# A kernel of 31 stages: one gathering of the five engines between two stages instead of two

## What is computed

```python
for l in range(2):
    h = rmsnorm(y, norm_mix_pre[l])
    m = mixer_ab(h) if l == 0 else mixer_cd(h)        # SSD heads + sparse attention / gated DeltaNet + dilated attention
    y = y + rmsnorm(m, norm_mix_post[l])
    y = y + rmsnorm(sq_relu_mlp(rmsnorm(y, norm_mlp_pre[l]), mlp_w1[l], mlp_w2[l]), norm_mlp_post[l])
```

## Time and profile before

| What | us |
|---|---|
| Median of three runs | 3000.59 |
| Lowest and highest of them | 2994.78, 3001.04 |
| Span of the profiled execution (first to last instruction) | 2999.4 |
| PE busy | 2651.9 (88%) |
| DVE, ACT, POOL busy | 1246.4, 951.2, 903.1 |
| Mean granted share of the TensorE clock | 0.927 |

### The profile page before, as it was taken

One profiled execution on the slowest core, in us unless ns is written; L12 is line 12 of the kernel. 1 busy time (PEld: TensorE's weight loads), 2 busy tenths in 40 slices (PEclk: granted clock), 3 DMA queues, 4 the chain that ended last, 5 costly groups with the idle time before them and its releaser, 6 DMA issues. The chain is left out here.

```text
span 2999.4 us, 47285 instructions
## 1 busy us (share of the span) xinstructions
PE 2651.9 (88%) x19663; PEld 2400.3 (80%) x19663; DVE 1246.4 (42%) x2527; ACT 951.2 (32%) x1755; POOL 903.1 (30%) x453
## 2 busy tenths in 40 slices
PE   5877889888889999978978897889998889899998
PEld 5745888555889999977967696779996569899997
DVE  5655411576343222252654365551105453522224
ACT  4242221364343212152432243222214543412122
POOL 2241221132254333352333133323330003533331
PEclk9978989898999999988988898889999889899998
DMA  4202255451122222222211020112322262122221
GB/s 147 74 15 77 82 93 129 141 214 58 43 71 71 85 85 85 85 74 62 71 31 30 17 76 26 31 30 73 104 73 73 60 185 89 60 85 77 79 84 60
DMA packets 217570, 232.93 MB, mean 78 GB/s; under 512 B 40780, under 2 KB 186668, under 8 KB 216750
## 3 DMA queue, kind: packets, MB, share of 16 engines
q1 hardware_dynamic: 215278, 229.66, 25.1%
q10 hardware_dynamic: 2080, 0.25, 0.1%
HBM read 207.93 MB, written 48.35 MB: 85 GB/s over the span
## 5 line engine op out<-in xcount | busy, mean ns | idle before, releaser
L271 POOL TENSOR_TENSOR WRr<-WR,WH 128x2048 fp32r<-128x2048 f32 (+3 forms) x98 | 438.3, 4472 | 855.0 <-ACT WH L259 855.0
L2231 PE MATMUL PS<-HHr,WRr 128*128 128x288 f32 x1104 | 327.7, 297 | 0.0
L411 PE MATMUL PS<-HHr,WH 128*128 128x288 f32 (+1 forms) x928 | 280.2, 302 | 41.9 <-PEq L97 41.9
L411 PE MATMUL PS<-YTr,WRr 128*128 128x288 f32 x1024 | 304.1, 297 | 0.0
L259 ACT CAST WH<-WR 128x2048 fp32r<-128x2048 f32 (+3 forms) x98 | 180.3, 1840 | 339.1 <-DMA WR<-in_mlp_w 187.6
L411 PE MATMUL PS<-YTr,lt_WX 128*128 128x288 f32 x1408 | 281.8, 295 | 0.0
L411 PE MATMUL PS<-HTr,WH 128*128 128x288 f32 (+1 forms) x928 | 278.1, 300 | 0.0
L411 PE MATMUL PS<-HHr,WRr 128*128 128x288 f32 (+1 forms) x928 | 278.0, 300 | 0.0
L271 POOL TENSOR_TENSOR WRr<-WR,lt_WX 128x2048 fp32r<-128x2048 f32 x35 | 162.1, 4630 | 234.0 <-ACT lt_WX L259 234.0
L411 PE MATMUL PS<-WH,HHr 128*128 128x256 f32 (+3 forms) x760 | 220.1, 290 | 13.0 <-PEq L97 13.0
L411 PEld LDWEIGHTS PS<-YTr,lt_WX 128*128 128x128 f32 x1408 | 227.1, 188 | 0.1
(11 more groups left out here) (672 smaller groups left out, 6145.6 us busy)
## 6 DMA issues: line engine op xcount, KB each, us to landing
WR<-in_mlp_w SPq DMA_DIRECT2D x64, 1024.0 KB, 5.3
WR<-in_cd_w_in SPq DMA_DIRECT2D x34, 1024.0 KB, 5.4
out_dil_s<-in_cache_dil_kv SPq DMA_DIRECT2D x2, 7936.0 KB
WR<-in_ab_w_in SPq DMA_DIRECT2D x10, 1024.0 KB, 5.4
past_rows<-in_cache_nsa_kv SPq DMA_DIRECT2D x16, 256.0 KB, 3.4
WR<-in_ab_w_in SPq DMA_DIRECT2D x16, 256.0 KB, 4.3
WR<-in_nsa_ck_w SPq DMA_DIRECT2D x4, 1024.0 KB, 5.6
WR<-in_nsa_cv_w SPq DMA_DIRECT2D x4, 1024.0 KB, 5.4
```

The costliest lines, as they stand in the source:

```text
L271: pool.tensor_tensor(K.WRr[:, n % RING, 0:used], K.WR[:, n % RING, 0:used], high_slot(K, i, used).bitcast(F32), ALU.subtract).then_inc(K.l ...
L411: last = pe.matmul(out, a, b, start=(n == 0), stop=(n == 3 * len(terms) - 1))
L2231: last = pe.matmul(out, a[:, k, c], h[:, k, x], start=(n == 0), stop=(n == 3 * KT - 1))
```

## The change

The clearing of a stage's semaphores moves from its end to the beginning of the next stage, after that stage has allocated its own, so the two sets never share one. The barrier behind the clearing goes. The block is opened without the option `no_gpsimd_drain`, so POOL drains too when the engines gather at its end. Behind the last stage the last set is cleared and one more barrier stands there, as before.

```diff
+SPENT = []
+
+
+def clear_spent(nc):
+    if SPENT:
+        nc.clear_and_free_semaphores(list(SPENT))
+        SPENT.clear()
+
+
 @contextmanager
 def stage(nc, *names):
     at = nc.next_id()
     sems = [nc.alloc_semaphore(f"{name}_{at}") for name in names]
-    with nc.Block(no_gpsimd_drain=True) as block:
+    clear_spent(nc)
+    with nc.Block() as block:
         yield (block, *sems)
-    nc.clear_and_free_semaphores(sems)
-    nc.all_engine_barrier()
+    SPENT.extend(sems)
...
 def build(nc, K, upto=99):
+    SPENT.clear()
     with ExitStack() as ctx:
...
         with stage(nc, "y_done") as (block, y_done):
...
                 for n in range(K.issued - RING, K.issued):
                     sp.wait_ge(K.w_landed[n % RING], landed(K, n))
+        clear_spent(nc)
+        nc.all_engine_barrier()
```

## The result

| | us |
|---|---|
| Before, median of 4 runs | 2999.41 (2994.78 to 3001.04) |
| After, median of 4 runs | 2972.47 (2970.15 to 2973.67) |
| Ratio, with its 95% interval | 0.9913 (0.9896 to 0.9930) |

The change makes the kernel 26.9 us (0.9%) faster. So the direction was right, and half of the gain was not foreseen. The profiled execution of after took 2971.89 us.

The account below looks back on a forecast made before the run. No single engine fills the span; every path crosses the stage ends, where all five engines wait for each other. 28 x (0.45 + 0.04) = 13.7 us off 3000.6 gives 2986.9 us, range 2981.0 to 2994.5.

Parts of the forecast that it names:

- the second gathering: At 30 of 31 stage ends it goes, saving 0.45 us from release to release; floor 0.37, ceiling 0.50.
- the merged step: At the first gathering, the drain counts the engine in itself, saving the last to arrive 0.04 us; bounds 0 and 0.08.
- the 28 handovers counted: Handovers where the gain arrives: 28 x (0.45 + 0.04) = 13.7 us, bounds 10.4 and 16.2.
- the form of the closing: At the block's end, taken to be line 97's, in which the drain counts the engine in itself; saves 0.04 us.
- the first handover and the last inner one: No gain at either: a DMA already in flight, small rows or the result's write, is what ends last.
- POOL's drain: At the block's close: cost 0 while POOL is not last to arrive, otherwise 0.04 to 0.08 us each.
- a set may be in two pieces: At the clearing, two live semaphore sets may mean two clears, 44 to 132 ns more, on POOL alone.
- each stage between its handovers as long as before: Inside the stages: a sign of being right, that their lengths between handovers stay unchanged.
- the clock had one sign: Rival at stage starts or ends: PE stays at the lower clock longer, using up the gain; 3010.7 us, chance 0.04.
- The rival with the clearing on the path: At stage starts, first needs wait for POOL's drain and clears, cutting the gain; taken as 2992 us, chance 0.15.
- the one in which the gain is waited out: In two thirds of stages a load or landing under way binds first; 9 handovers pay, 2996.2 us, chance 0.09.
- more than I say, for the clock's sake: Whole kernel: a gain above the forecast, through the clock or the merged step; 2980 us, chance 0.04.

Follow-up runs that it names:

- e2: Changed kernel with a second gathering put back behind the clearing at all 30 handovers: 3006.54 us, beside 3000.23 for the kernel before.
- e3: Changed kernel with a second gathering put back at 28 handovers, all but those into `nsa_sample` and `dilated_sample`: 2998.72 us.
- e4: Changed kernel with a second gathering put back only at the two handovers into `nsa_sample` and `dilated_sample`: 2976.30 us.
- e12: Kernel before the change, unedited, profiled a second time: `nsa_sample` took 42.3 us; the kernel before was timed at 2994.27 us in that set.
- e14: Kernel before the change, unedited, profiled a fourth time: `nsa_sample` took 42.3 us; the kernel before was timed at 2994.27 us in that set.
- e5: Changed kernel with two empty gatherings at the start of `nsa_prompt` and two at that of `dilated_prompt_heads`: 2982.77 us.
- e9: Kernel before the change with seven empty gatherings added at the start of `nsa_prompt`: 2999.53 us, beside 2996.65 for the kernel before.
- e10: Kernel before the change with seven empty gatherings added at `nsa_prompt` and six at `dilated_prompt_heads`: 3012.09 us, beside 2996.65 for the kernel before.
- e11: Changed kernel with two empty gatherings added ahead of `ssd_tiles`, a delay of 0.8 us: 2975.67 us.
- e7: Changed kernel with eight empty gatherings at the start of `nsa_prompt` and eight at that of `dilated_prompt_heads`: 2985.50 us.
- e1: Changed kernel, unedited, run and profiled again: 2972.86 us.
- e8: Changed kernel with one gathering at the first 11 handovers and two at the later 19: 2987.95 us.
- e6: Changed kernel with four empty gatherings at the start of `nsa_prompt` and four at that of `dilated_prompt_heads`: 2990.45 us.

## Why the prediction was half right

**Right, in mechanism and nearly in size:** the price of a handover. I took 0.45 us for the second gathering and 0.04 for the merged step, 0.49 together; 0.52 was measured, within the bounds (0.37 to 0.58). How it divides between the two no run shows. For the 28 handovers counted, that is 14.7 us against 13.7.

**Right:** the form of the closing was that of line 97; the first handover and the last inner one gave nothing, each for the reason given; ACT's first act at the handover of `ssm_gate` came after 0.28 us, inside the 0.25 to 0.35 foretold. **Right in effect, wrong in size:** POOL's drain. I had 40 to 81 ns for it and named one over 0.1 us as a sign of being wrong; it has a median of 4.6 us. It cost nothing, for the reason given: POOL was never the last to arrive.

**Right in place, wrong in number:** "a set may be in two pieces". It was up to four, 65 clears in all. e2 shows their price when they are on the path: its 29 handovers cost 3.8 us more than those of before.

**Wrong: "each stage between its handovers as long as before".** The whole sum 2999.4 - 13.7 rests on it. The list of bounds had terms for the price of a handover and for the spread of runs, and none for the stages' lengths. Three stages moved by 4 to 9 us in the first pair of profiles, and by the means of the profiles the stages gave 12 us beside the 15 of the handovers. The mean granted clock went from 0.927 to 0.932, a sign of being wrong that the prediction itself named.

**Wrong in the rivals: the clock had one sign.** The rival priced it well (5 us at the lower level cost 2.4 us) and placed it at stage starts, but let it only take back the gain, since "the change shortens idle stretches and adds none". The runs show that it is not the shorter idle stretch right ahead that counts (e3, e4, e12, e14) but where the stage starts against the changes of the clock, which a shift of the timeline moves and which can go either way. It was shown for `nsa_sample` and `ssd_sample`, in which PE has short bursts and waits. A range for a change that shifts the timeline by 15 us should have held both signs of this: the 17 profiles of this study, handovers taken out, lie between 2960 and 2981 us, 21 us apart, and before alone between 2970 and 2978.

**The rival with the clearing on the path** and the one in which the gain is waited out both predicted less than measured, and the handovers' rows exclude them. The Trainium skill (Runtime: NRT & Kernel Launch, section "The ~15µs preamble/postamble breakdown") gives some 355 ns for the runtime's own walk over the five engines, which no run here shows; here one gathering less, with its merged step, was 0.52 us.

**The case "more than I say, for the clock's sake"** named the right cause and had 0.04; its 2980 was still 7.5 us too slow.

**What stays open:** whether the 12 us belong to this change in any deeper sense. They are steady for this kernel (2970.15 to 2973.98 over nine runs), and both its profiles have `nsa_sample` start in the same place against the clock's changes; why its executions differ so little and those of before so much is not shown. e5 lost about 8 of the 12 us to 2 us of empty gatherings, so the next edit may lose them too. For `dilated_sample`, the largest part, and for the 3.0 us elsewhere the clock is a fit of the numbers and not shown as the cause. Nor was the rule found by which the clock falls at one change and not at another; my aim in e9, e10 and e11 missed. A stage with the clock held high was not tried.

## What to carry to other kernels

A gathering of five engines costs about half a microsecond here (0.39 to 0.56 us each for the empty ones of e5 to e7), and nothing in the busy shares shows it; count the gatherings, and read one from end to start in the timeline. Work that only tidies up, like clearing semaphores, cost nothing here once nobody waited behind it, and in e2, scattered as it now is, more than before where somebody did. For any change that shifts the timeline of a kernel with low-clock stretches, take several profiles of both sides and split the gain into the part that was removed and the part that the clock moved: only the first can be counted on behind the next edit.

## What the runs showed of the hardware

- `nsa_sample`, with the same instructions, took 42.3 us in seven of the 17 profiles, 49.3 to 50.0 in six, 51.2 in two, and 52.7 and 58.1 once each. The granted share was 0.91 for the shortest and 0.67 for the longest.
- What decides its length is where it starts against the changes of the granted clock: the first fall came 17.2 to 17.5 us after its start in the seven short ones, 2.0 to 3.2 us after it in the others. With delays of 1.1, 1.8 and 3.1 us ahead of the 165 us stage before it, one profile each, it took 49.3, 51.2 and 42.4 us.
- Executions of different kernels fall into the same lengths to a few hundredths of a microsecond (42.36, 42.32, 42.36, 42.34, 42.34 in after, e1, e7, e8, e11). The spread between runs differs by kernel: 3.8 us in nine runs of after, 17 us in 22 of before, 23.5 us in ten of e6.
- A POOL drain behind its own running operation took up to 6.4 us and ended 0.05 to 0.07 us after that operation; an idle one took 40 ns.
